# High parts of a half panel first, then its low parts: the order of matmuls in a panel with stationary weights

## What is computed

```python
proj = rms_norm(x, norm_w) @ w_in                      # (256, 2048) @ (2048, 10272), and others like it
x = x + concatenate([y_a, y_b, y_m], -1) @ w_out
q = (rms_norm(c_q, mla_q_norm_w) @ mla_w_uq)
q, k, v, g = split(h @ w_in, ...)                      # retention
```

## Time and profile before

| | us |
|---|---|
| median of 3 runs | 2,735.02 |
| lowest, highest | 2,733.7, 2,735.73 |
| the profiled execution | 2,736.33 |
| its span | 2,734.8 |
| PE busy (share of span) | 2,687.5 (98%) |
| PEld busy | 2,306.0 (84%) |
| DVE busy | 1,895.1 (69%) |
| ACT busy | 1,395.4 (51%) |

### The profile page before, as it was taken

One profiled execution on the slowest core, in us unless ns is written; L12 is line 12 of the kernel. 1 busy time (PEld: TensorE's weight loads), 2 busy tenths in 40 slices (PEclk: granted clock), 3 DMA queues, 4 the chain that ended last, 5 costly groups with the idle time before them and its releaser, 6 DMA issues.

```text
span 2734.8 us, 42970 instructions
## 1 busy us (share of the span) xinstructions
PE 2687.5 (98%) x14638; PEld 2306.0 (84%) x14638; DVE 1895.1 (69%) x2950; ACT 1395.4 (51%) x2081; POOL 60.9 (2%) x84
## 2 busy tenths in 40 slices
PE   8999999999998999999999999999999999999998
PEld 7888888887887888888888888888888888888886
DVE  6766678887767677777777656666777576575664
ACT  5544466665555555565555545454554344343443
POOL 0000000000000111100000000000000000000000
PEclk9999999999999999999999999999999999999999
DMA  7755465545673445566555555555555655555553
GB/s 272 217 185 186 168 217 173 188 173 174 183 251 118 137 143 164 178 185 217 171 186 173 182 187 172 173 187 175 185 180 198 199 185 184 197 184 189 192 187 127
DMA packets 120005, 502.18 MB, mean 184 GB/s; under 512 B 9168, under 2 KB 9296, under 8 KB 82032
## 3 DMA queue, kind: packets, MB, share of 16 engines
q1 hardware_dynamic: 115456, 480.28, 52.8%
q0 software_dynamic: 4032, 20.03, 2.2%
q10 hardware_dynamic: 432, 0.74, 0.1%
HBM read 492.58 MB, written 8.43 MB: 183 GB/s over the span
## 4 chain that ended last, share of the span: by engine, by line
PE 80%; issue 9%; DVE 4%; ACT 3%; DVEq 2%; POOL 1%; DMA 1%; ACTq 0%; SPq 0%; POOLq 0%
PE pj L1697 36%; PE pj L1700 18%; PE pj L1724 7%; PE pj L1728 7%; PE pj L1727 7%; ACT w_hi L491 1%; DVE w_lo L891 1%; POOL gen L456 1%; PE pj L2138 1%; PE mx L2096 1%; PE pj L1877 1%; PE mx L1742 1%; PE pj L2141 0%; PE mx L2114 0%; PE mx L1918 0%
## 5 line engine op out<-in xcount | busy, mean ns | idle before, releaser
L891 DVE TENSOR_TENSOR w_lo<-raw,w_hi 128x1024 fp32r<-128x1024 f32 (+1 forms) x1010 | 1132.6, 1128 | 493.1 <-ACT w_hi L491 480.5
L491 ACT ACTIVATE w_hi<-raw 128x1024 fp32r<-128x1024 f32 (+1 forms) x1010 | 983.9, 979 | 736.6 <-PE pj L1697 394.9
L1697 PE MATMUL pj<-hs,w_hi 128*128 128x512 f32 x3792 | 1350.9, 400 | 5.6 <-DVE xT L904 4.6
L1700 PE MATMUL pj<-hs,w_lo 128*128 128x256 f32 x3792 | 1062.8, 280 | 0.0
L1697 PEld LDWEIGHTS pj<-hs,w_hi 128*128 128x128 f32 x3792 | 712.9, 188 | 178.2 <-DVE xT L904 5.0
L1700 PEld LDWEIGHTS pj<-hs,w_lo 128*128 128x128 f32 x3792 | 716.5, 189 | 2.2 <-issue 1.0
L1697 PE MATMUL pj<-ys,w_hi 128*128 128x512 f32 x1328 | 473.1, 401 | 7.5 <-DVE ys L911 3.9
L1700 PE MATMUL pj<-ys,w_lo 128*128 128x256 f32 x1328 | 374.0, 282 | 0.0
L496 ACT ACTIVATE half<-pj 128x256 f32<-128x256 f32 x371 | 141.0, 380 | 403.5 <-PE pj L1700 382.2
L1697 PEld LDWEIGHTS pj<-ys,w_hi 128*128 128x128 f32 x1328 | 250.9, 189 | 71.3 <-DVE ys L911 4.7
L1700 PEld LDWEIGHTS pj<-ys,w_lo 128*128 128x128 f32 x1328 | 252.2, 190 | 0.0
(11 more groups left out here) (341 smaller groups left out, 2031.4 us busy)
## 6 DMA issues: line engine op xcount, KB each, us to landing
raw<-in_w_up SPq DMA_DIRECT2D x64, 1024.0 KB, 4.9
raw<-in_w_down SPq DMA_DIRECT2D x64, 1024.0 KB, 5.7
raw<-in_w_ssd SPq DMA_DIRECT2D x48, 1024.0 KB, 4.8
raw<-in_w_ret_a SPq DMA_DIRECT2D x48, 1024.0 KB, 4.8
raw<-in_w_ret_b SPq DMA_DIRECT2D x48, 1024.0 KB, 4.8
raw<-in_w_out SPq DMA_DIRECT2D x64, 640.0 KB, 3.9
raw<-in_w_gate SPq DMA_DIRECT2D x32, 1024.0 KB, 4.9
raw<-in_w_mem SPq DMA_DIRECT2D x16, 1024.0 KB, 7.1
```

The costliest lines, as they stand in the source:

```text
L491: A(hi, w, ACT.Copy).then_inc(hi_ready, 1)
L891: TT(lo, w, hi.bitcast(F32), ALU.subtract).then_inc(split_ready, 1)
L1697: ins = mm(pj[:, k], w_hi[:, s + h, u], m, start=opens and t == 0, stop=False)
L1700: ins = mm(pj[:, k, 0:T], w_lo[:, s + h, u], m[:, 0], start=False, stop=closes and t == order[-1])
```

## The change

In `panel`, the loop over tiles becomes a loop over the two halves; in each, first the high parts of all its tiles are issued, and then their low parts. `late` tiles go with the second half. The waits (`split_ready`, `before`), the `mid` functions and `half_started` stay with the high part of their tile. The number, the operands and the lengths of the matmuls are the same.

```diff
-                    for t in order:
-                        m = moving[t]
-                        h = int(at + t >= half_)
-                        u = at + t - h * half_
-                        if h and u == 0:
-                            pe.wait_ge(split_ready, c.half(j, 1))
-                        if at + t in mid:
-                            mid[at + t]()
-                        if at + t in before:
-                            pe.wait_ge(*before[at + t])
-                        ins = mm(pj[:, k], w_hi[:, s + h, u], m, start=opens and t == 0, stop=False)
-                        if u == 0 and not (h and late):
-                            ins.then_inc(half_started, 1 if h else started)
-                        ins = mm(pj[:, k, 0:T], w_lo[:, s + h, u], m[:, 0], start=False,
-                                 stop=closes and t == order[-1])
+
+                    for g in (0, 1):
+                        mine = [t for t in order if int(at + t >= half_) == g and not (g == 0 and t in late)]
+                        if g:
+                            mine += list(late)
+                        for t in mine:
+                            h = int(at + t >= half_)
+                            u = at + t - h * half_
+                            if h and u == 0:
+                                pe.wait_ge(split_ready, c.half(j, 1))
+                            if at + t in mid:
+                                mid[at + t]()
+                            if at + t in before:
+                                pe.wait_ge(*before[at + t])
+                            ins = mm(pj[:, k], w_hi[:, s + h, u], moving[t], start=opens and t == 0, stop=False)
+                            if u == 0 and not (h and late):
+                                ins.then_inc(half_started, 1 if h else started)
+                        for t in mine:
+                            h = int(at + t >= half_)
+                            u = at + t - h * half_
+                            ins = mm(pj[:, k, 0:T], w_lo[:, s + h, u], moving[t][:, 0], start=False,
+                                     stop=closes and t == order[-1])
```

## The result

The changed kernel takes 2,738.61 us (median of 20 runs, 2,735.48 to 2,744.15), the kernel before 2,732.86 us in 20 runs beside them (2,726.48 to 2,737.31). The ratio is 1.0025 with a 95% interval of 1.0018 to 1.0032: slower by a quarter of a per cent, where I had forecast 2,730 and gave 0.42 to faster, 0.35 to the same and 0.23 to slower. Of all the runs reported here two took about twice the time, one of the kernel before (5,495 us) and one of e4 (5,378 us), and are left out.

The account below looks back on a forecast made before the run. TensorE was taken to bound the kernel, by its matmul pace and few waits. Pace -25.2, switches +5.4, waits +13.5 and pace lost ahead of waits +1.5 gave -4.8 us, so 2,730 us, range 2,714 to 2,747.

Parts of the forecast that it names:

- signs of being wrong: Low stream above 120 ns, a half paying more than 25 ns for switches, or waits not growing as worked out.
- the pace term: TensorE's matmul pairs: sorted streams run at 346.7 ns a pair, gaining up to 25.2 us; switches take back 5.4.
- What bounds the kernel, the streams: TensorE's matmul pace and waits bound it; streams of one length run at 226.5 ns (512 columns) and 119.6 ns (256).
- The switches: Two changes of matmul length per half of a panel, taken at 8 ns a half, 5.4 us; bounds 0 to 17.
- The number of long pairs: In the profiled run 3,780 of 4,844 undisturbed pairs take about 353 ns, losing 25.2 us over 346.7 ns.
- The waits inside panels: TensorE reaches mid blocks and operand waits sooner while producers do not: 13.5 us lost, bounds 7 to 16.
- L781's slack: MLA's value product comes 0.48 us earlier, its producer L781 ends just in time; 0.7 us if short by 0.1.
- rival 3: Lengthened SSD waits drop TensorE to 1.2 GHz; four drops cost 6 us, bringing 2,736 us; chance 0.08.
- The sum: Whole kernel: -25.2 + 5.4 + 13.5 + 1.5 = -4.8 us, against the median 2,735.0 giving 2,730.2.
- Rival 2: Order makes no difference to pace, only the waits ahead of mid blocks remain: 2,748.5 us, slower; chance 0.16.

Follow-up runs that it names:

- e4: Kernel before with the new order except in halves waiting for an operand, called blocks placed where TensorE comes as late as before; 2,725.08 us, ratio 0.9978 to before.
- e1: The changed kernel again, no edit, beside the kernel before: median 2,735.81 us over 12 runs against 2,731.33, ratio 1.0023.
- e5: The kernel before again, no edit, for a second trace of it: 2,733.1 us.
- e6: The kernel before again, no edit, for a third trace of it: 2,729.7 us.
- e8: As e4, but the second half of a panel runs low parts first, then high parts; 2,722.22 us, ratio 0.9946 to the kernel before.
- e10: As e8, with the SSD value product, MLA scores and retention's value product called later than in the kernel before; 2,712.64 us, ratio 0.9933 to before.

## Why the prediction was wrong

The mechanism was right, a better pace against longer waits, and none of the signs of being wrong that I had named came: the low stream takes 120 ns, a half pays less than 25 ns for its switches, and the waits grew nearly as worked out. What failed is the size of the pace term, and the clock that I left out of the sum. I had forecast that the pace wins 19.8 us (25.2 less 5.4) against 15.0 of waits. It wins 14.6 between the first two traces and 11.3 or 8.3 from the other two of before, while waits and other grow by about 14.

- *What bounds the kernel, the streams.* Right: 227 and 120 ns inside the streams, in every trace.
- *The switches.* This step failed: 8 ns a half taken, 20 measured, so that the sorted order keeps 13.2 us of lost pace in place of 5.4. The rows for it stood in the prediction: 25 ns over five intervals, and 28 were measured, less the 8 that the low parts give back. I set them aside for the 6.7 ns of a long pair, which is not a switch between streams.
- *The number of long pairs.* This step failed too, as a size. "A gain of up to 25.2 us" was the loss of the one profiled run, which has 3,788 long pairs; the two other traces have 3,324 and 2,860, and 3 and 6 us less to win. That run was at the upper end of before's, and I corrected for 1.3 us, the distance to a median of three, where 20 runs show 3.5.
- *The waits inside panels.* Right in mechanism and nearly in size: waits and other grew by 13.7 us between the profiles, 15.0 were predicted (13.5, and 1.5 of pace that is lost ahead of waits). Call by call, from start to start of the matmuls, the growth is 4.3, 2.1, 2.6, 3.2, 1.7, 0.3 and 0.0 us (retention's value product, MLA scores, SSD product, SSD statistic, square sums, retention's statistic, MLA values) for 3.8, 1.9, 1.9, 3.4, 1.5, 0.3 and 0. L781's slack, "just enough", was enough: its weight loads wait longer (2.2 us in place of 1.0), its matmuls don't.
- *The clock*, rival 3. It came beside the forecast and not in its place: the changed kernel's 20 runs have their median 3.1 us above a run with a mean clock of 0.996, and its traces have 6.0 low stretches on average against 4.7. I had given it 0.08 as a case that excludes the others; it should have been a term of the sum, of 0 to 3 us, since in e1 the median run has a clock of 0.996 and is 4.5 us above before all the same.
- *The sum* with e5, a run at the median of before's 20, is -11.3 (24.5 to 13.2) + 13.0 + 0.8 = +2.5 us to the changed kernel's first trace, and their runs differ by 2.4. With e6, the quickest of the three, it is -8.3 + 13.4 + 0.6 = +5.7. To the +2.5 the median adds the 3.1 us of clock, which comes near the measured 5.8. How much of that is clock and how much is the number of long pairs differs between the series, and the runs don't separate the two.
- *Rival 2*, the one on the other side, had the right sign and the right place (the waits ahead of the calls decide), but not its cause: the order does change the pace. The Trainium skill ("TensorE: Matmul & The Clock Gate", section "Back-to-back issue gap"), named beside it, gives the gap of an isolated matmul by its columns alone. For the streams here that is not borne out: the same 512 columns take 227 to 241 ns by what stands ahead.

That the time still falls in the range of 2,714 to 2,747 is no merit of the sum, which had the sign wrong.

## What to carry to other kernels

When instructions of an in-order engine are sorted, look at what is called between them: everything that waits is reached sooner by all that was moved behind it, and where its producer has no slack each such microsecond is lost in full. Place those calls by time, not by the index of the loop; here that turned +0.25% into -0.2% (e4). Low parts first in the second halves brought another 3 us (e8), and letting three calls come as late as their producers finish another 9 (e10), -0.7% in all. Before a gain of a few tenths of a per cent is read off one trace, see that the trace is of a usual run: in this kernel the quantity that was to be gained differed by 6 us between three runs at a mean clock of 0.995 to 0.996.

## What the runs showed of the hardware

- Pairs of a 512- and a 256-column matmul with a weight load each have two steady paces at the upper clock, 346.7 and 353.3 ns, that last for long stretches and fall out differently from run to run of the same program (3,788, 3,324 and 2,860 long pairs). Sorted streams have one, a half in 2,793 ns.
- A switch from 256 to 512 columns costs 28 ns, spread over the next five matmuls (233, 236, 228, 233, 231 against 227 ns); in the other direction the first two intervals are 8 ns shorter together (113 and 119 against 120). The two make 20 ns, and in e8, with one of each less in a panel, two halves take 5,567 ns in place of 5,586.
- At the lower clock a pair takes 640 ns (427 and 213), just 768 columns at 1.2 GHz, where at the upper one 27 to 33 ns stand on top of 320.
- Of the 20 lengthened waits in the SSD phase in five traces of the changed kernel (1.9 to 2.2 us), 6 were followed by 3.4 us at 1.2 GHz: the first, of 2.2 us, in four traces of five, the other three, of 1.9, in 2 of 15. Of the 12 in the traces of before (1.2 to 1.5 us) none was.
